# The first block's gather in a mixture of experts: from the start of the expert stage to the end of the routing stage, without its copy of the indices

## What is computed

```python
x = x + attention(rmsnorm(x))                      # layer 0 windowed, layer 1 differential
x2 = rmsnorm(x)                                    # 1024 tokens x 1024, float32
g = argmax(x2 @ w_group)                           # top-1 of 4 groups
top_i, weights = top2(softmax((x2 @ w_router)[g])) # 2 of the 8 experts of that group
# tokens are sorted by expert and padded into blocks; each block has one expert
for each block:
    xb = x2[rows of the block]
    y  = (silu(xb @ w_gate[e]) * (xb @ w_up[e])) @ w_down[e]     # 1024 -> 512 -> 1024
out = scatter-add of weight * y;   x = x + out
```

## Time and profile before

| | us |
|---|---|
| median of 3 runs | 2630.5 (2630.07 to 2634.17) |
| the profiled execution | 2631.06 |
| its span | 2629.4 |
| PE busy in the span | 2330.4 (89%) |
| DVE, ACT, POOL busy | 1869.7, 1552.1, 282.9 |
| mean granted TensorE clock | 0.951 |

### The profile page before, as it was taken

The page is one execution under the profiler, slowest core; times in us unless marked ns, Lnnn a source line. Parts: engine busy times, 40 slices in busy tenths (PEclk is TensorE's granted clock), DMA queues, the critical chain, the costliest instruction groups (busy, mean ns, idle before and its releaser), DMA issues. The chain is left out here.

```text
span 2629.4 us, 34467 instructions
## 1 busy us (share of the span) xinstructions
PE 2330.4 (89%) x11464; PEld 1758.9 (67%) x11464; DVE 1869.7 (71%) x2461; ACT 1552.1 (59%) x2036; POOL 282.9 (11%) x260
## 2 busy tenths in 40 slices
PE   7899989569999999929999999998955999999991
PEld 6666658447777777727777777776844777777671
DVE  5775572668898888858556666556256888888895
ACT  5554460447777777735555565555043778777772
POOL 0000020012121111030000000002001122211102
PEclk9999999779999999959999999999977999999996
DMA  3012020469999999852000000002146999999995
GB/s 121 25 55 96 24 72 32 170 227 397 392 395 399 402 394 395 338 174 89 24 24 24 24 24 24 0 24 72 32 171 206 390 394 401 398 394 393 403 360 212
DMA packets 129501, 538.48 MB, mean 205 GB/s; under 512 B 23232, under 2 KB 52032, under 8 KB 80288
## 3 DMA queue, kind: packets, MB, share of 16 engines
q1 hardware_dynamic: 110496, 470.62, 47.1%
q0 software_dynamic: 18944, 67.12, 7.3%
HBM read 487.50 MB, written 50.20 MB: 204 GB/s over the span
## 5 line engine op out<-in xcount | busy, mean ns | idle before, releaser
L1507 DVE TENSOR_TENSOR m_lo_gate<-m_raw_gate,m_hi_gate 128x2048 fp32r<-128x2048 f32 x132 | 298.9, 2290 | 81.7 <-ACT m_hi_gate L1502 79.8
L1507 DVE TENSOR_TENSOR m_lo_up<-m_raw_up,m_hi_up 128x2048 fp32r<-128x2048 f32 x128 | 292.5, 2285 | 7.1 <-ACT m_hi_up L1502 7.0
L1507 DVE TENSOR_TENSOR m_lo_down<-m_raw_down,m_hi_down 128x2048 fp32r<-128x2048 f32 x124 | 280.2, 2283 | 13.7 <-ACT m_hi_down L1502 13.7
L1502 ACT CAST m_hi_down<-m_raw_down 128x2048 fp32r<-128x2048 f32 x124 | 236.2, 1907 | 90.7 <-DMA m_raw_down<-in_moe_w_down_dram 54.8
L1502 ACT CAST m_hi_gate<-m_raw_gate 128x2048 fp32r<-128x2048 f32 x132 | 247.8, 1908 | 25.6 <-DMA m_raw_gate<-in_moe_w_gate_dram 25.4
L1502 ACT CAST m_hi_up<-m_raw_up 128x2048 fp32r<-128x2048 f32 x128 | 244.4, 1911 | 22.2 <-DMA m_raw_up<-in_moe_w_up_dram 21.2
L1622 PE MATMUL m_G<-m_hi_gate,m_x_hi 128*96 128x512 f32 x512 | 206.1, 402 | 11.4 <-DVE m_x_lo L1732 11.3
L1622 PE MATMUL m_U<-m_hi_up,m_x_hi 128*96 128x512 f32 x512 | 205.2, 401 | 0.0
L1623 PE MATMUL m_G<-m_hi_gate,m_x_lo 128*96 128x512 f32 x512 | 204.6, 400 | 0.0
L1624 PE MATMUL m_G<-m_lo_gate,m_x_hi 128*96 128x512 f32 x512 | 202.5, 395 | 0.0
L1623 PE MATMUL m_U<-m_hi_up,m_x_lo 128*96 128x512 f32 x512 | 201.8, 394 | 0.0
(11 more groups left out here) (380 smaller groups left out, 4907.9 us busy)
## 6 DMA issues: line engine op xcount, KB each, us to landing
m_raw_gate<-in_moe_w_gate_dram SPq DMA_DIRECT2D x128, 1024.0 KB, 11.1
m_raw_up<-in_moe_w_up_dram SPq DMA_DIRECT2D x128, 1024.0 KB, 12.8
m_raw_down<-in_moe_w_down_dram SPq DMA_DIRECT2D x124, 1024.0 KB, 12.0
out_rows<-m_y POOLq DMA_DIRECT2D x64, 384.0 KB, 7.5
a1n_rows<-in_diff_w_qkv_dram SPq DMA_DIRECT2D x21, 512.0 KB, 5.5
out_rows<-a0n_gain SPq DMA_DIRECT2D x1, 8064.0 KB, 37.3
x_res<-in_x_dram SPq DMA_DIRECT2D x4, 1024.0 KB, 9.6
a0n_rows<-in_swa_w_o_dram SPq DMA_DIRECT2D x8, 512.0 KB, 3.3
```

The source lines that it names most:

```text
L1502: act.copy(self.hi[w][:, cut], self.raw[w][:, cut]).then_inc(self.hi_done[w], 1)
L1507: eng.tensor_tensor(self.lo[w][:, cut], self.raw[w][:, cut], self.hi[w][:, cut].bitcast(F32), ALU.subtract)\
```

## The change

The gather of block 0 leaves `Experts.run` and becomes POOL's last instruction of the routing stage. It waits until all stores into `hn_rows` have landed, and for a new semaphore `listed` that DVE raises when the table is written. It takes its row numbers straight from column 0 of the table, without the copy to `pick`. For this `xg` and the semaphore `gathered` are allocated before the routing stage (`gathered` as one that is not cleared between layers, with a name for each layer), and the tile `owner_cmp` of the routing stage now lies in the first scratch tile of the normalization, whose contents are no longer needed then. In the expert stage POOL begins with `gather(1)`. The other engines' lists are as they were, but that DVE's last instruction of the routing stage raises `listed` instead of `own`.

```diff
+    def lasting_sem(self, name):
+        return self.nc.alloc_semaphore(name=name)
...
-        owner_cmp, ctl_f = v("owner_cmp", (COLS - EXPERTS) * EXPERTS), v("ctl_f", COLS + 1)
+        owner_cmp, ctl_f = norm.junk[:, 0:(COLS - EXPERTS) * EXPERTS], v("ctl_f", COLS + 1)
...
+        listed = s("listed")
...
                 pool.affine_select(out=below[:, :], in_=ones[:, :], compare_op=ALU.is_gt, fill=0.0, base=0,
                                    pattern=[[1, P]], channel_multiplier=-1).then_inc(made, 1)
+
+                for stored in norm.rows_stored:
+                    pool.wait_ge(stored, 16 * NT // norm.bufs)
+                pool.wait_ge(listed, 1)
+                moe.gather(pool, moe.table[:, 0:1])
...
-                own(dve.tensor_copy(moe.table[:, :], L_ps[0:CAP, 0, 0:COLS]))
+                dve.tensor_copy(moe.table[:, :], L_ps[0:CAP, 0, 0:COLS]).then_inc(listed, 1)
...
+        self.xg = sb(f"{name}_xg", [CAP, D], F32)
+        self.gathered = t.lasting_sem(f"{name}_gathered")
...
+    def gather(self, pool, rows):
+        pool.indirect_dma_start(out=self.xg[:, :], out_offset=None, in_=self.hn_rows,
+                                in_offset=bass.IndirectOffsetOnAxis(rows, 0)).then_inc(self.gathered, 16)
...
                     def gather(b):
-                        if not (isinstance(b, int) and b == 0):
-                            pool.wait_ge(gathered, 16 * b)
+                        pool.wait_ge(gathered, 16 * b)
                         pool.tensor_copy(pick[:, :], ...).then_inc(picked, 1)
-                        if not (isinstance(b, int) and b == 0):
-                            pool.wait_ge(x_turned, b)
-                        wait_apart(pool, picked, b + 1, pick_seen)
-                        pool.indirect_dma_start(out=xg[:, :], ...).then_inc(gathered, 16)
+                        pool.wait_ge(x_turned, b)
+                        wait_apart(pool, picked, b, pick_seen)
+                        self.gather(pool, pick[:, :])
...
-                    for b in range(4):
+                    for b in range(1, 4):
                         gather(b)
-                        if b >= 3:
-                            store(b - 3)
+                    store(0)
```

More of the change, by code:

```diff
@@ L1036, in _ @@
                 own(dve.tensor_copy(ctl_f[:, 1:1 + EXPERTS], count_up[:, 0:EXPERTS]))
-                owners = owner_cmp[:, :].rearrange("p (b e) -> p b e", e=EXPERTS)
+                owners = owner_cmp.rearrange("p (b e) -> p b e", e=EXPERTS)
                 own(tt_(owners, running[:, :].unsqueeze(1).broadcast_to((P, COLS - EXPERTS, EXPERTS)),
@@ L1519, in run @@
             hi, lo, lo_done = self.hi, self.lo, self.lo_done
-            pick = sb(f"{name}_pick", [CAP, 1], I32)
-            xg = sb(f"{name}_xg", [CAP, D], F32)
+            pick, xg, gathered = sb(f"{name}_pick", [CAP, 1], I32), self.xg, self.gathered
             x_hi, x_lo = sb(f"{name}_x_hi", [P, KD * CAP], F32R), sb(f"{name}_x_lo", [P, KD * CAP], F32R)
@@ L1530, in run @@
             gate_done, up_done, down_done = s("gate_done"), s("up_done"), s("down_done")
-            picked, gathered, x_turned, x_hi_done, x_lo_done = s("picked"), s("gathered"), s("x_turned"), s("x_hi"), s("x_lo")
+            picked, x_turned, x_hi_done, x_lo_done = s("picked"), s("x_turned"), s("x_hi"), s("x_lo")
             gated_done, hid_done, h_turned, h_hi_done, h_lo_done = s("gated"), s("hid"), s("h_turned"), s("h_hi"), s("h_lo")
@@ L1583, in gather @@
                     def gather(b):
-                        if not (isinstance(b, int) and b == 0):
-                            pool.wait_ge(gathered, 16 * b)
+                        pool.wait_ge(gathered, 16 * b)
                         pool.tensor_copy(pick[:, :], self.table[:, b:b + 1] if isinstance(b, int) else self.table[:, bass.ds(b, 1)])\
                             .then_inc(picked, 1)
-                        if not (isinstance(b, int) and b == 0):
-                            pool.wait_ge(x_turned, b)
-                        wait_apart(pool, picked, b + 1, pick_seen)
-                        pool.indirect_dma_start(out=xg[:, :], out_offset=None, in_=self.hn_rows,
-                                                in_offset=bass.IndirectOffsetOnAxis(pick[:, :], 0)).then_inc(gathered, 16)
+                        pool.wait_ge(x_turned, b)
+                        wait_apart(pool, picked, b, pick_seen)
+                        self.gather(pool, pick[:, :])
                     def store(b):
```

## The result

| | before | after |
|---|---|---|
| median | 2630.28 us (4 runs) | 2610.82 us (4 runs, 2610.06 to 2612.75) |
| ratio of the runs | | 0.9924 (0.9908 to 0.9940) |
| the profiled execution | 2631.06 | 2610.06 |
| its span | 2629.4 | 2608.2 |

The time fell by 19.5 us, as forecast. The way in which it fell was not the one forecast: the number came out right by luck. First the page of the changed kernel: busy time of the engines, and the granted clock in 40 slices. It differs little from the earlier trace rows: one slice of each pair of sevens has become 8.

A forecast was written before the change was run, and what follows sets the result against it. PE's longest stall per layer's expert stage, the first gather's rows, was taken as the bound. Gains of 10.08 + 9.90 = 19.98 us from 2631.06 gave 2611.08, 2610.52 against the median; forecast 2611.0, range 2608 to 2620.

The forecast's parts named there:

- Earlier issue: Start of block 0's gather on POOL: issued 0.26 us after the table, at 533.86; other bound 0.94 us.
- Issue time: POOL issuing the first gather: 0.93 us, as DVE has just finished; 2.19 us as the other end.
- Landing: First gather's rows: land 3.99 us after issue, at 537.85, with no transfer running at issue; other bound 10.50 us.
- The barrier moves: Barrier after the routing stage: opens 1.19 us later (0.26 + 0.93), moving ACT's split, DVE's instructions and SP's loads.
- What is late next: First `x_lo`: at 539.94, still set by the gather's rows, DVE free at 539.85; gain 10.08 and 9.90 us per layer.
- The tiles that move: `xg` in SBUF and `owner_cmp` in the scratch tile: no instruction's size changes, so an effect of nothing.
- Downstream: After the first turn: block 1's weights fit into 6.4 us of idle DMA; the second gather is hidden by 1.3 us.
- Rival 1: First gather meets the weights and lands 10.50 us after issue: 2624.1; chance 0.09 including what lies between.
- Rival 2: Gate matmuls come earlier but all run at 1.2 GHz: 2618.8; chance 0.09.
- Rival 3: The weight stream is the bound and the later barrier delays it: 2633.4, or 2637.5 if slower; chance 0.07.
- Rival 4: POOL stands in a wait for something else, so rows come no earlier; at 14 us all as before, 2631; chance 0.03.
- The clock: First gate product: counted as nothing; bounds 3.8 us per layer more or 1.9 us less.

The follow-up runs named there:

- the repeat: The changed kernel run once more with no edit: 2613.0 us (6 runs), ratio 0.9933.
- the experiment above: Kernel before, with a plain store of 512 KB or 4 MB added as POOL's last routing-stage instruction, its landing awaited only at the expert stage's end; no time given.
- the version with 2.51: Kernel before, with block 0's gather as POOL's first expert-stage instruction, straight from the table without the copy: 2624.63 us (11 runs), ratio 0.9982.
- that with 4.43: Changed kernel, with DVE's second half of `lo_gate` and first half of `lo_up` moved into the routing stage, ACT doing `x_hi` first: 2619.43 us, ratio 0.9963.

## Why the forecast came out right, and where its steps failed

The number was right (2611.0 forecast, 2610.8 measured, 2613.0 in the repeat) by luck: two errors have opposite signs.

- **Earlier issue.** I took 0.26 us for POOL's wait and kept 0.94 as the other bound. Measured 0.92 and 0.85: the other bound. Why is not shown. That POOL had stood in the wait for 64 us is not enough as a reason, as the plain stores of the experiment above started 0.30 to 0.32 us after the table behind a wait as long. The stores into `hn_rows` had long landed (the last was issued by 490.5 and none took more than 7.6 us), so their waits cost nothing, as reasoned.
- **Issue time.** 0.93 forecast, 1.08 and 0.95 measured. Right, and for the reason given: beside DVE it was 2.51 and 4.43. This agrees with what the Trainium skill ("GPSIMD Engine Reference", Key points) says of the shared interfaces, and 4.43 against 1.07 is its price here. What counts is who comes first: an issue that began while DVE was in a split of `raw` and `hi` ended 0.8 to 1.0 us after the end of such a split (2.19, 2.51 and 4.43 us), and one that began together with a split took 0.95 us (543.62 against 543.61 in the version in which DVE waits for the issue). Why of two splits in a row only the first held it in the version with 2.51, and both in that with 4.43, is not shown.
- **Landing.** 3.99 forecast. In the changed kernel the landing stands in the traces at 4.1 us in the first and 3.9 in the repeat; without a barrier behind it, the turn came 4.23 us after the issue's start (5.52 against 1.29). Right within 0.3.
- **The barrier moves.** This is the step that failed. I let it move by POOL's wait and issue, 1.19 us; it moved by 4.85 (5.38 against 0.53) and 4.74. I had the barrier wait for the end of the issue; it waits until POOL's DMA has landed, which the stores of 512 KB and 4 MB show.
- **What is late next.** With DVE's chain behind that barrier, `x_lo` came at 9.81 us after the table, not 6.34. I had named DVE's two instructions as second by 0.09 us; with the real barrier they are first by 2.3. The version with both instructions out of the way shows it: `x_lo` follows the turn by 2.06 us. With only the second half of `lo_gate` out of the way it still starts as `lo_up` ends (542.68 and 542.76), but 2.1 us sooner after the table. Both versions also have ACT do `x_hi` first, so DVE's share isn't parted from ACT's, which was 0.3 us smaller. Gain of the turn: 6.5 and 6.6 us per layer instead of 10.08 and 9.90, 6.9 us less than forecast.
- **The tiles that move.** I wrote "nothing". Alone they gave a ratio of 0.9992 and 0.9977, 2 and 6 us by the middle values, and with them the slow blocks are gone in 13 of 14 layers. This is the second failed step, of the other sign. In the sum of the text's own terms, 13.1 of the turn and some 4 of the places make 17, near the 17.6 us of the repeat.
- **Downstream.** The second block's gather was hidden as reasoned: its rows were there at 549.46, the turn came at 554.19. The later start of the loads cost nothing seen.
- **Rival 1** (the gather meets the weights) didn't happen, but its mechanism is real: 10.55 us beside weights issued together with it. I counted on an order in time, 2.25 us ahead. Whether that lead would have been enough was not tried, as the barrier in fact keeps the loads away for the whole landing. The rule of the Trainium skill that I had set against this rival ("DMA: Bandwidth & Descriptors", section "SWDGE vs HWDGE vs iDMA": turns between the queues) does show here, and I read the trace of before wrongly on it: once the gather's packets ran, they went about one for one with those of the weights (27 to 24 in one microsecond). What was wrong is what I drew from it, that a few early weights would cost about nothing.
- **Rival 2** (the clock takes it back) didn't happen: from the first gate matmul to `gated` it took 7.49 and 7.26 us in the first trace of after, against 7.39 and 7.92 before, with a granted clock of 0.76 and 0.78 against 0.77 and 0.71.
- **Rival 3**: the barrier is indeed late, by more than its point of decision (2.6 us per layer), and the kernel is no slower. The end of the stage isn't set by the weights' first issue.
- **Rival 4** (POOL held by something else) didn't happen beyond the 0.92 us above.
- **The clock.** I counted nothing for the first gate product, with -3.8 to +7.7 us as bounds, and that was right. At another place the clock makes up steps of 1.57 us in the traces: the last down product of a layer follows a wait of 1.89 us, and in some executions the granted clock then falls to 1.2 GHz within it. In the first trace of before, layer 0, the change in the midst of the product (0.39 and 0.63 us are a matmul at 2.4 and at 1.2 GHz; the granted clock is 1.00 up to 1121, 0.50 from 1122 to 1124 and 1.00 again from 1125):

```profile
1119.69 0.47 PE L1622 MATMUL m_Y<-m_hi_gate,m_h_hi 128*96 128x512 f32 x1 [1.89 <-DVE m_h_lo L1737]
1120.91 0.39 PE L1624 MATMUL m_Y<-m_lo_gate,m_h_hi 128*96 128x512 f32 x1
1121.53 0.63 PE L1623 MATMUL m_Y<-m_hi_gate,m_h_lo 128*96 128x512 f32 x1
1124.79 0.39 PE L1622 MATMUL m_Y<-m_hi_gate,m_h_hi 128*96 128x512 f32 x1
```

This was so in 3 of the 4 layers of before's two traces and in none of after's. So of the 6.5 us that the two stretches of blocks gave in the table above (means of two traces), 2.4 are this (3 times 1.57 over 2), and 3.8 are the time from the first silu to the last, which holds the slow blocks. But the version with the gather before the barrier and the second half of `lo_gate` moved had it in both layers, the one without a barrier behind the gather in one, with the same instructions and the same wait at that place. Over all traces it stands in 6 of 14 layers with the tiles in the old places and in 4 of 14 with the new ones. I take it for chance; it isn't shown. The block that follows the first also took 18.83 instead of 17.3 to 17.6 us in one layer of each of these two, while PE's instructions were the same. In the first of them the granted clock was 0.50 there from 561 to 567, behind PE's wait of 4.01 us for `x_lo`.

## What to carry to other kernels

A DMA that is issued last before a barrier isn't a DMA that runs on behind it: find out whether the engine at the barrier is held until it has landed, and then put work for the other engines beside it or put it behind the barrier. A small transfer that everybody waits for is best given the DMA engines for itself; here that meant not to ask for the large ones until it had landed. And a change that looks like bookkeeping, where tiles lie, is to be timed alone before its effect is booked to the rest.

## What the runs showed of the hardware

- POOL is held at the end of a stage until its DMA has landed. From the table to the opened barrier: 3.77 us with 512 KB, 13.18 with 4 MB, 5.38 with the gather, 0.53 without a DMA, with the opening 0.3 to 0.4 us behind the landing.
- A gather of 0.39 MB landed 3.9 to 4.2 us after its start where no weights ran and DVE left the issue alone, 5.2 to 5.6 and 7.3 to 7.7 where DVE stretched the issue to 2.2 to 2.5 and 4.4 us, which is 2.8 to 3.3 us after the issue's end each time. The first gather beside 3 MB of weights took 9.9 to 10.6, whether it was issued 2.51 us behind them or 0.04 us ahead.
- The gather's issue is stretched by a DVE split of `raw` and `hi` that is already running: 2.19 to 2.51 and 4.43 us against 0.93 to 1.08. It took 0.93 beside `x_lo`, and 0.95 beside a split that began with it.
- The same instructions ran faster with tiles at other places in SBUF, 2 us (not clear of noise) and 6 us in two sets of runs, by blocks of 17.63 instead of 17.8 us at the end of each layer. Why is open.
